# Modulation pieces moved out of the mixers of a diffusion step into the routing stretches behind them

## What is computed

```python
for i in range(DEPTH):                                   # 4 layers: attn, mlstm, gla, attn
    sc1, ac1, gc1, sc2, ac2, gc2 = adaln(c_ctx, w_mod[i], b_mod[i])   # silu(c) @ w_mod + b_mod, six vectors
    sl1, al1, gl1, sl2, al2, gl2 = adaln(c, w_mod[i], b_mod[i])
    hc = rmsnorm(xc, norm1_g[i]) * (1 + ac1) + sc1       # the same for xl
    yc, st = mixer(hc, ...)
    xc = xc + gc1 * yc
    hc2 = rmsnorm(xc, norm2_g[i]) * (1 + ac2) + sc2
    xc = xc + gc2 * moe(hc2, router_w, router_b, moe_wg[i], moe_wu[i], moe_wd[i])   # 16 experts, top 2
y_prompt, y_sample = rmsnorm(xc, final_g), rmsnorm(xl, final_g)
```

## Time and profile before

| | us |
|---|---|
| median of 3 runs | 1785.13 |
| lowest and highest run | 1782.42, 1789.11 |
| the profiled execution, its own time | 1786.43 |
| span of its profile | 1784.6 |
| TensorE busy in the span | 1697.7 (95%) |
| TensorE's granted clock, mean | 0.979 |

### The profile page before, as it was taken

How to read it: one execution, slowest core, us unless ns; L and a number is a source line. 1 busy time by engine, 2 the same in 40 slices (tenths; PEclk the granted TensorE clock), 3 DMA queues, 4 the chain that set the end, 5 groups by cost and what they waited for, 6 DMA issues and landing times.

```text
span 1784.6 us, 21218 instructions
## 1 busy us (share of the span) xinstructions
PE 1697.7 (95%) x8603; PEld 979.9 (55%) x8603; DVE 466.6 (26%) x1245; ACT 368.7 (21%) x749; POOL 37.9 (2%) x49
## 2 busy tenths in 40 slices
PE   5999999999999999999998999999999999999996
PEld 3577544436744887734434657844443787444443
DVE  2142511105304220411112154431111353410112
ACT  2132300003133620400002124310000342100001
POOL 1000000000000000000000000000000000000000
PEclk9999999999999999899999999999999999999998
DMA  9989699999997249499999697689999738799993
GB/s 357 382 287 385 273 428 428 427 427 342 372 336 281 97 167 384 162 424 428 428 429 397 254 357 282 250 335 427 428 428 418 276 113 360 296 428 428 428 428 143
DMA packets 134763, 612.11 MB, mean 343 GB/s; under 512 B 12485, under 2 KB 19285, under 8 KB 109576
## 3 DMA queue, kind: packets, MB, share of 16 engines
q1 hardware_dynamic: 117408, 589.84, 82.4%
q10 hardware_dynamic: 12824, 12.85, 2.2%
q0 software_dynamic: 4432, 8.02, 1.2%
HBM read 608.81 MB, written 8.94 MB: 346 GB/s over the span
## 4 chain that ended last, share of the span: by engine, by line
PE 82%; DMA 11%; DVE 3%; ACT 2%; issue 1%; SPq 1%; ACTq 0%; DVEq 0%
PE PS L1580 22%; PE PS L1007 21%; PE PS L1591 11%; PE PS L1544 7%; DMA ring<-in_moe_wg 6%; PE PS L1037 4%; PE PS L1093 3%; DVE arena L2144 2%; DMA out_C<-small 2%; DMA ring<-in_attn_w_qkv 1%; PE PS L1524 1%; PE PS L1061 1%; DMA ring<-in_w_mod 1%; PE PS L1585 1%; PE PS L1529 1%
## 5 line engine op out<-in xcount | busy, mean ns | idle before, releaser
L1580 PE MATMUL PS<-ring,arena 128*64 128x512 f32 x1280 | 367.6, 594 | 7.6 <-DMA ring<-in_moe_wg 7.6
L941 ACT ACTIVATE arena<-PS 128x512 f32<-128x512 f32 (+1 forms) x130 | 70.7, 544 | 804.9 <-PE PS L1571 343.7
L1580 PEld LDWEIGHTS PS<-ring,arena 128*64 128x64 f32 x1280 | 115.6, 137 | 185.1 <-issue 183.9
L1007 PE MATMUL PS<-HS,ring 128*128 128x256 f32 x896 | 199.4, 380 | 0.0
L2144 DVE TENSOR_TENSOR arena<-arena,PS 128x512 f32<-128x512 f32 x32 | 33.5, 1048 | 613.2 <-PE PS L1580 613.2
L1007 PEld LDWEIGHTS PS<-HS,ring 128*128 128x128 f32 x896 | 168.9, 190 | 27.4 <-issue 5.1
L1580 PE MATMUL PS<-arena 128*64 128x512 f32 x576 | 169.7, 594 | 0.4 <-DMA arena<-in_moe_wg 0.4
L1544 PE MATMUL PS<-arena 128*128 128x256 f32 (+3 forms) x688 | 144.6, 361 | 5.9 <-ACT arena L941 3.7
L1591 PE MATMUL PS<-ring,arena 128*64 128x512 f32 x640 | 146.0, 607 | 2.5 <-DVE arena L2125 2.5
L1544 PEld LDWEIGHTS PS<-arena 128*128 128x128 f32 (+1 forms) x688 | 112.2, 190 | 44.9 <-issue 22.7
L1007 PE MATMUL PS<-arena,ring 128*128 128x256 f32 x512 | 114.5, 384 | 2.1 <-ACT arena L690 1.1
(11 more groups left out here) (338 smaller groups left out, 1523.5 us busy)
## 6 DMA issues: line engine op xcount, KB each, us to landing
ring<-in_w_mod SPq DMA_DIRECT2D x48, 2048.0 KB, 16.7
ring<-in_moe_wu SPq DMA_DIRECT2D x41, 2048.0 KB, 22.1
ring<-in_moe_wd SPq DMA_DIRECT2D x41, 2048.0 KB, 23.1
ring<-in_moe_wg SPq DMA_DIRECT2D x41, 2048.0 KB, 21.5
arena<-in_moe_wg SPq DMA_DIRECT2D x24, 2048.0 KB, 20.8
HS<-in_moe_wu SPq DMA_DIRECT2D x12, 2048.0 KB
arena<-in_moe_wu SPq DMA_DIRECT2D x12, 2048.0 KB, 22.1
arena<-in_moe_wd SPq DMA_DIRECT2D x12, 2048.0 KB, 26.7
```

Of the source, the lines that this page charges most:

```text
L941: A(dst, src, func).then_inc(S(sem), 1)
L1007: ins = mm(out, a, b, start=first and i == 0, stop=final and i == len(pairs) - 1)
L1580: ins = mm(PS[64 * e:64 * e + 64, b, :], XG[:, k, 64 * e:64 * e + 64], w[:, k], start=(k == 0), stop=(k == KD - 1))
```

## The change

`MODS` now has nine groups, of 4, 9, 3, 12, 3, 9, 3, 4 and 1 pieces. Groups 1, 3, 5 and 7 stand in the mixers, groups 2, 4, 6 and 8 behind them: ten pieces. The mixers of layers 0, 1 and 2 lose 3, 4 and 3 pieces; the last keeps four. A group behind a mixer adds up in bank 6 and is copied to the tile `RS`. Its first piece takes the place of the 4 fillers, its second runs in two halves inside the logits, its third takes the place of the filler before the gather, and two of the 3 fillers behind the transposes go. In layer 3 the group has one piece, which takes the place of the 4 fillers; the 3 stay. The gather of pair 0 goes to banks 0 and 1. `mod_cols` of the group stands behind the `wg` products of pair 0. The chunks of these pieces are issued between the mixer's last chunk and the first of the experts, so they hold ring slots that chunks 6, 7 and 8 of the experts go to.

```diff
-MODS = [ORDER[a:b] for a, b in ((0, 4), (4, 16), (16, 32), (32, 44), (44, 48))]
-GMODS = (0, 2, 4, 6, 8, 10, 12)
+MODS = [ORDER[a:b] for a, b in ((0, 4), (4, 13), (13, 16), (16, 28), (28, 31), (31, 40), (40, 43), (43, 47), (47, 48))]
+GMODS = (0, 2, 4, 5, 6, 8, 9)
+        chunks += mod(behind_mixer(l))
         chunks += [(w, l, p + NPAIR * e) for p in range(NPAIR) for w in ("wg", "wu", "wd") for e in range(2)]
...
-                    if q == (7, 5, 7, 3)[l]:
+                    if q == (6, 5, 6, 3)[l]:
                         early()
+                    if q == SPARE + RING - 1:
+                        sp.wait_ge(S("ht"), 4 * (l + 1))
+                        load(n + SPARE - 1)
                     load(n + q)
-                sp.wait_ge(S("ht"), 4 * (l + 1))
-                load(n + SPARE - 1)
...
+            def mod_rows(g, i, ks=range(KD)):
+                if i >= len(MODS[g]):
+                    return
...
                     for s in range(2):
                         ins = mm(bank(4 + s, 0, NE), H[:, k, T * s:T * s + T], RW[:, k], start=(k == 0), stop=(k == KD - 1))
+                    if k in (2, 5):
+                        mod_rows(gb, 1, range(4) if k == 2 else range(4, KD))
...
-                warm(WARM[2])
+                warm(1 if len(MODS[gb]) > 2 else WARM[2], 7)
...
-                warm(WARM[3])
+                mod_rows(gb, 2)
                 pe.wait_ge(S("pw"), 36 * l + 4)
-                gather(BANKS[1], "gather")
+                gather((0, 1), "gather")
...
                 sumsq(2 * l + 1)
-                warm(WARM[1])
+                mod_rows(behind_mixer(l), 0)
```

More of the change, by code:

```diff
@@ L106, with in_mixer, behind_mixer, mod_group @@
 ORDER = [(l, c) for l in range(DEPTH) for c in range(12)]
-MODS = [ORDER[a:b] for a, b in ((0, 4), (4, 16), (16, 32), (32, 44), (44, 48))]
-GMODS = (0, 2, 4, 6, 8, 10, 12)
+MODS = [ORDER[a:b] for a, b in ((0, 4), (4, 13), (13, 16), (16, 28), (28, 31), (31, 40), (40, 43), (43, 47), (47, 48))]
+def in_mixer(l):
+    return 2 * l + 1
+def behind_mixer(l):
+    return 2 * l + 2
+def mod_group(l, c):
+    return next(g for g, group in enumerate(MODS) if (l, c) in group)
+GMODS = (0, 2, 4, 5, 6, 8, 9)
 def mod_parts(g):
@@ L133, in plan_chunks @@
     chunks = []
-    mod = lambda l, lo, hi: [("mod", l, c) for c in range(lo, hi)]
-    chunks += mod(0, 0, 4)
-    chunks += [("qkv", 0, 2)] + mod(0, 4, 8) + [("qkv", 0, 0)] + mod(0, 8, 12) + [("qkv", 0, 1)] + mod(1, 0, 4)
+    mod = lambda g, lo=0, hi=12: [("mod", *u) for u in MODS[g][lo:hi]]
+    chunks += mod(0)
+    chunks += [("qkv", 0, 2)] + mod(1, 0, 4) + [("qkv", 0, 0)] + mod(1, 4, 5) + [("qkv", 0, 1)] + mod(1, 5, 9)
     chunks += [("wo", 0, 0), ("wo", 0, 1)]
@@ L141, in plan_chunks @@
                 chunks += {4: [("c0", 1, 0)], 8: [("mz", 1, 0)]}.get(c, [])
-                chunks += [("min", 1, c)] + ([("mod", *u) for u in MODS[2][2 * c:2 * c + 2]] if c < 8 else [])
+                chunks += [("min", 1, c)] + (mod(3, 2 * c, 2 * c + 2) if c < 4 else mod(3, 4 + c, 5 + c) if c < 8 else [])
             chunks += [("mout", 1, (c, r)) for c in range(2) for r in range(2)]
@@ L323, in program @@
         YSS, YR = sm(0, 2, 2), sm(8, 2)
-        MP = [ar(8000, 512), ar(8000, 512), ar(8192, 512), sq(1536, 512), ar(8000, 512)]
+        RSF = RS[:, :, :].rearrange("p a b -> p (a b)")
+        MP = [ar(8000, 512), ar(8000, 512), RSF, ar(8192, 512), RSF, sq(1536, 512), RSF, ar(8000, 512), RSF]
+        MB = [7 if g % 2 or g == 0 else 6 for g in range(len(MODS))]
         QT = ar(0, 8, N2)
@@ L1029, in _ @@
             after(pe, "cs")
-            def mod_rows(g, i):
+            def mod_rows(g, i, ks=range(KD)):
+                if i >= len(MODS[g]):
+                    return
                 l, c = MODS[g][i]
                 w = landed(pe, POS["mod", l, c])
-                for k in range(KD):
+                for k in ks:
                     r = 32 * (k % 4)
-                    ins = mm(PS[r:r + 32, 7, :], CS[:, k, 30 - 2 * i:62 - 2 * i], w[:, k], start=(i == 0 and k < 4), stop=(i == len(MODS[g]) - 1 and k >= 4))
-                ins.then_inc(S("mod_rows"), 1)
+                    ins = mm(PS[r:r + 32, MB[g], :], CS[:, k, 30 - 2 * i:62 - 2 * i], w[:, k], start=(i == 0 and k < 4), stop=(i == len(MODS[g]) - 1 and k >= 4))
+                if k == KD - 1:
+                    ins.then_inc(S("mod_rows"), 1)
             def mod_run(g, lo, hi):
@@ L1277, in mlstm @@
                         scores(1)
-                mod_cols(2)
+                mod_cols(in_mixer(1))
                 def turn(u):
@@ L1493, in gla @@
                 output(1)
-                mod_cols(3)
+                mod_cols(in_mixer(2))
                 output(2)
@@ L1614, in pair @@
                             slot_id()
+                            mod_cols(gb)
                         if not first and g == 0:
```

63 lines of the change are left out of this document (34 added, 29 removed).

## The result

| | before | changed |
|---|---|---|
| median of 8 runs, us | 1784.16 | 1796.97 |
| lowest and highest | 1781.69, 1789.11 | 1792.11, 1800.37 |
| ratio, with its 95% interval | | 1.0079 (1.0064 to 1.0094) |
| the profiled execution, and its span | 1786.43, 1784.6 | 1793.7, 1791.9 |

The change costs 12.8 us; 1786 was forecast, in a range up to 1795.

The account below looks back on a forecast made before the run. DMA and TensorE were taken as nearly balanced, with DMA setting each layer's end from chunk 9 on. Layer terms of +3.1, −5.8, +3.5 and 0 summed to +0.8 us, giving 1786 us, in a range of 1772 to 1795.

Parts of the forecast that it names:

- From chunk 9 on DMA sets a layer's end: Each layer's experts: time is the mixer up to its end, then the time to chunk 9, then a constant.
- The sign that was named for it: Last pair of layers 0 and 2: TensorE's wait longer than 1.9 us by some 4 to 5 us.
- the wait for HS: Pair 0 of layers 0 and 2: TensorE waits 3 to 5 us, adding nothing to the stream's own delay.
- Layers 0 and 2: Mixers shorter by 5.4 and 4.6 us, chunk 9 later behind them by 8.5 and 8.1; together +3.1 and +3.5.
- Rival B: Stream behind the mixers of layers 0 and 2 runs at 387 GB/s, not 426: 1794 us; chance 0.12.
- Layer 1: Mixer loses four pieces, −7.1 us; the way behind it grows by 1.3; together −5.8.
- In these chunk 9 moves only with TensorE's way to the gather: Layers 1 and 3, behind the mixer: late loads stay hidden, by 3.3 and 2.6 us.
- Behind E in layer 1: From the mixer's end (issue of the last ring load) to the gather: +1.3 us, between −0.5 and +4.9.
- Layer 3: Mixer keeps its pieces and one piece replaces 4 fillers behind it: 0 us.
- The sum: All four layers: +0.8 us on the profiled execution's 1786.43, given as 1786 us for the median.
- the rivals: Late loads not setting the end, 1772, chance 0.22; slower stream, 1794, 0.12; mixers not getting shorter, 1795, 0.06.
- the chance for slower: Whole kernel above the upper bound of 1794.1 us: 0.14.

Follow-up runs that it names:

- e1: The changed kernel with the two arena loads one place earlier in layers 0 and 2; 1785.3 us, ratio 1.0011 to the kernel before.
- d7: The changed kernel with the arena loads one place later in layers 0 and 2, behind chunk 6; 1796.3 us, ratio 1.0066.
- e2: The changed kernel with SyncE's two arena loads of layer 1 held until the mLSTM's state is written out; 1786.2 us, ratio 1.0013.
- e3: The changed kernel with arena loads one place earlier in layers 0 and 2, and layer 1's held until the state is written; 1775.2 us, ratio 0.9946.
- b1: The kernel before, with only layer 1's arena loads, and what is behind them, held until the state is written; 1781.0 us, ratio 0.9975.
- h1: The changed kernel with layer 1's arena loads two places earlier and no wait added; 1798.8 us, ratio 1.0103.
- c2: e3 with three fillers behind the transposes again, where the change left one; 1771.2 us, ratio 0.9934.
- g1: e3 with the second piece whole ahead of the logits and three fillers behind the transposes; 1765.7 us, ratio 0.9909.
- h2: g1 with layer 1's arena loads two places earlier in place of the wait for the state; 1774.3 us, ratio 0.9964.

## Why the prediction was wrong

- **"From chunk 9 on DMA sets a layer's end": right as far as the sum used it.** The change, e1 and d7 are ordered as their chunk 9 is. But TensorE had less slack than was thought. The sign that was named for it, a wait at the last pair longer by 4 to 5 us in layers 0 and 2, didn't come (1.7 us, and none). TensorE's own way to the gather had grown by 4.9 and 3.3 us (17.3 to 22.2, 17.8 to 21.1), and the wait for HS took 1.1 and 2.5 more.
- **Layers 0 and 2: right.** By the packets chunk 9 starts 9.4 and 9.0 us later against E (forecast 8.5 and 8.1). The mixers are shorter by 6.7 and 4.5 (5.4 and 4.6): layer 0's E moves from 174.17 to 167.44, layer 2's by 4.39, to 1140.90, from a first piece that moved 0.12 the other way. Rival B's rate, 387, was too low and 426 a little too high: 411. The Trainium skill's 358 GB/s for a core, "DMA: Bandwidth & Descriptors", Specifications, bounds nothing here: the trace has 411 to 428 GB/s where the stream is back to back.
- **Layer 1: wrong, and this is the step that failed.** "In these chunk 9 moves only with TensorE's way to the gather" took it that the way starts at the mixer's end. It asked of a mixer that ends earlier only what TensorE and the chunk stream do, and never what else must be finished by then. The mixer did get shorter, by 12.6 us even (E 10.96 earlier from a start 1.68 later) instead of 7.1, in part because TensorE no longer waited 2.87 and 0.69 for ScalarE's late copies of the state, which it did in the trace of before. Then it stood 10.2 us for a state write. Layer 1 gave +2.1 in place of −5.8. Two changes met there: E came earlier, and the arena loads moved from 668.5 to 696.5, because their place in the queue is behind piece chunks and ring loads that now wait for slots. The sum for the moved steps counted SyncE's queue, but not ScalarE's, whose writes share DMA with it. The trace of before had the sign. Its chain from 660 to 760 has a state write as its longest link of DMA, issued behind five of the experts' chunks:

```profile
677.28 27.05 DMA out_C<-small
```

- **Behind E in layer 1: mis-sized.** The term was +1.3, with ends of −0.5 and +4.9. From the first sums to the gather the kernel before takes 20.1 us (722.74 to 742.85). e2 and e3, where TensorE doesn't wait for the state, take 22.5 (710.07 to 732.60) and 23.4 (704.89 to 728.30): +2.4 and +3.3. In e3 the copy of ScalarE is 2.0 later, as reckoned (1.8), but the third piece, taken at full clock, 1.8, runs at half, 3.58. In e2 it runs at full clock, as it does in the change (1.92, at 744.78), and the logits with the halves in them take 9.0 us, not 6.2 + 1.8. The granted clock of the stretch is 0.75 before, 0.77 in e2 and 0.71 in e3. So the pieces in halves didn't raise it, and whether they lower it these runs don't decide.
- **Layer 3: nearly right.** From E to chunk 9 28.4 for 28.68. Its mixer's end came 2.9 late, of which 2.6 is the wait at its start, below.
- **The sum.** With the 11.8 us of e2 taken off, the change stands at 1.0013 of before, +2.3 us; +0.8 was forecast. That is partly luck: the hold takes 4.5 us off the kernel before as well, and against b1 e2 is at +7 us. So the collision with the state writes is the largest part of the miss, and some 6 us beside it (layer 1's way behind the mixer, and more that was not traced to a stage) were hidden by a fault that before had too. Of the rivals none was it; the chance for slower, 0.14, came for the most part from a stream rate and mixers that weren't what happened.

## What to carry to other kernels

When work is taken out of a stage, list everything that must be finished at the stage's end on every queue, writes to HBM among them, and see how much slack each had: here a last write that had cost nothing became 10 us of wait. A small write beside megabytes of prefetch moves one of its packets for one of the prefetch's. Hold the loads until it is out if something waits for it, and judge it by what is still to be moved, not by the time of issue. Count the chunks that a change leaves behind a serial point: moving two loads one place in an in-order queue was worth 12 us, where all the pieces that were moved had been reckoned at 17. And before a gain is put down to an edit, look in the traces whether it lies where the edit is.

## What the runs showed that was not expected

**A small write goes packet for packet with the loads.** In the kernel before, from 670 to 720, the 128 KB state writes have medians of 5.4 and 3.6 us from issue to landing. The medians hide the four that were issued first, from 672 to 678, beside the experts' chunks: they took 13.4 to 27.1, and the last six, with no load beside them, 1.9 to 2.0. From 676 to 701 there are 628 packets of 16 KB and 672 of 512 B. In the change the last write has 21.55, in h1 one has 24.16.

**A busy TensorE at a lowered clock.** From E to the release of chunk 9 in layer 0 of the change TensorE was busy for 30.60 of 32.90 us, at a granted clock of 0.84. The Trainium skill ("TensorE: Matmul & The Clock Gate", Part 1) lets activity release the throttle; the prediction took pieces among 128x16 logit matmuls for such activity, and layer 1's term would have come out lower still by it. The runs speak against that reading of it for pieces in halves (0.77 and 0.71, against 0.75 before). Two whole pieces ahead of the logits had 0.91.

**A wait at a layer's start that moves about.** TensorE's first sums of layer 2 or 3 stand up to 4 us with nothing in the profile to wait for, and then often run at half clock. It is at layer 2 in the kernel before; at layer 3 in the change (2.60 us, put down to ScalarE, whose squares had begun 3.8 us earlier) and in all its variants with one filler, e3 above among them; in c2, g1 and h2, with three fillers, it falls into the sums of layer 2. Before, and c2:

```profile
970.92 6.21 PE L1061 MATMUL PS<-HS,consts 128*128 128x256 f32 x16 [4.22 <-issue]
```

```profile
956.48 4.54 PE L1084 MATMUL PS<-HS,consts 128*128 128x256 f32 x12 [3.08 <-issue]
```

In the profiled pair this hides the cost of layer 1's longer experts (5.7 us late at their end, 0.12 late at the first piece of layer 2) and adds 2.6 in layer 3. The packets point to the fetching of TensorE's instructions: in all 13 traces TensorE goes on 2.5 to 2.8 us after a 16 KB packet starts on a queue that the profile calls `instruction` (968.1 in the kernel before, 1368.3 in e3, 954.0 in c2). No run tests it. That the wait moves between kernels is a reason to compare medians and not two profiles, and to look where a difference of two profiles lies.
